# Two attention stages of a two-block transformer: the matmuls of an even and an odd head put next to each other in TensorE's queue

## The reference

```
# block 1: LayerNorm, projection, two attentions of 8 heads each (head width 64), gated mix
s = einsum('bwhd,bkwjhd->bhwkj', q, k_neighbours) * scale + bias     # neighbourhood, 8 heads
s = where(|i-j| <= 128, q.k * scale, -1e30); softmax with a sink logit  # windowed, 8 heads
mixed = sigmoid(ga) * (y_na @ w_na) + sigmoid(gb) * (y_swa @ w_swa)
# then FFN (4096), pooling mixer, convolutional GLU FFN (2816)
# block 2: 16 query heads on 4 key/value heads, causal window of 128, sinks
p = softmax(where(valid, q.k * scale, -1e30) with sink);  o = p @ v;  o @ w_o
# then a second convolutional GLU FFN
```

## Time and profile before

| | |
|---|---|
| median of 3 runs | 1015.7 us (1015.56 to 1016.41) |
| profiled execution | span 1013.8 us from the first to the last instruction; no time of its own is listed beside the span |
| PE busy | 925.0 us, 91% of the span |
| DVE, ACT, POOL busy | 652.8, 476.3, 191.3 us |
| chain that ended last | PE 77%, DVE 14% |
| stage 1 of attention | about 79.8 to 168.2 us |
| stage 2 of attention | about 707.1 to 772.2 us |

### The profile page before, as it was taken

The page is one execution under the profiler, slowest core; times in us unless marked ns, Lnnn a source line. Parts: engine busy times, 40 slices in busy tenths (PEclk is TensorE's granted clock), DMA queues, the critical chain, the costliest instruction groups (busy, mean ns, idle before and its releaser), DMA issues.

```text
span 1013.8 us, 17618 instructions
## 1 busy us (share of the span) xinstructions
PE 925.0 (91%) x7016; PEld 877.8 (87%) x7016; DVE 652.8 (64%) x864; ACT 476.3 (47%) x669; POOL 191.3 (19%) x166
## 2 busy tenths in 40 slices
PE   5898999979999999678999999869998699999995
PEld 5897878879999999568999999858677699999994
DVE  6636554767455454757776767587764867667675
ACT  4554464325444444344655454452555355545541
POOL 0501120025000000233121212431230411212131
PEclk9999999988999999778999999979899799999996
DMA  9651233443554555212454545315212145545411
GB/s 291 238 206 43 83 125 126 151 163 125 189 185 166 181 191 188 102 42 84 150 194 175 190 168 200 126 61 188 84 43 84 63 150 204 189 176 180 175 67 42
DMA packets 21842, 146.69 MB, mean 145 GB/s; under 512 B 2336, under 2 KB 3488, under 8 KB 4640
## 3 DMA queue, kind: packets, MB, share of 16 engines
q1 hardware_dynamic: 21648, 145.44, 40.2%
q10 hardware_dynamic: 144, 0.56, 0.2%
HBM read 144.94 MB, written 1.05 MB: 144 GB/s over the span
## 4 chain that ended last, share of the span: by engine, by line
PE 77%; DVE 14%; ACT 3%; issue 3%; DMA 2%; POOL 1%; DVEq 0%; ACTq 0%; SPq 0%; POOLq 0%
PE up L885 15%; PE up L886 14%; PE up L887 14%; PE down L885 7%; PE down L886 7%; PE down L887 7%; PE down L1024 3%; DVE w_lo L1311 2%; DVE region L1676 2%; DMA w<-w_stream 2%; PE down L1045 1%; DVE x_lo L1548 1%; PE aux L1045 1%; PE down L1034 1%; ACT w_hi L603 1%
## 5 line engine op out<-in xcount | busy, mean ns | idle before, releaser
L885 PE MATMUL up<-x_lo,w_hi 128*128 128x256 f32 x1360 | 391.8, 288 | 9.1 <-DVE w_lo L1311 8.7
L886 PE MATMUL up<-x_hi,w_hi 128*128 128x256 f32 x1360 | 387.1, 285 | 0.0
L887 PE MATMUL up<-x_hi,w_lo 128*128 128x256 f32 x1360 | 387.0, 285 | 0.0
L1311 DVE TENSOR_TENSOR w_lo<-w,w_hi 128x2048 fp32r<-128x2048 f32 x130 | 298.8, 2300 | 87.3 <-ACT w_hi L603 87.1
L603 ACT ACTIVATE w_hi<-w 128x2048 fp32r<-128x2048 f32 x134 | 254.9, 1904 | 74.9 <-PE down L887 42.2
L885 PEld LDWEIGHTS up<-x_lo,w_hi 128*128 128x128 f32 x1360 | 263.1, 193 | 20.3 <-DVE w_lo L1311 9.9
L886 PEld LDWEIGHTS up<-x_hi,w_hi 128*128 128x128 f32 x1360 | 263.4, 194 | 0.0
L887 PEld LDWEIGHTS up<-x_hi,w_lo 128*128 128x128 f32 x1360 | 263.3, 194 | 0.0
L885 PE MATMUL down<-mid_lo,w_hi 128*128 128x256 f32 x608 | 173.9, 286 | 10.0 <-DVE mid_lo L1685 10.0
L886 PE MATMUL down<-mid_hi,w_hi 128*128 128x256 f32 x608 | 173.4, 285 | 0.0
L887 PE MATMUL down<-mid_hi,w_lo 128*128 128x256 f32 x608 | 173.3, 285 | 0.0
(11 more groups left out here) (182 smaller groups left out, 971.8 us busy)
## 6 DMA issues: line engine op xcount, KB each, us to landing
w<-w_stream SPq DMA_DIRECT2D x134, 1024.0 KB, 4.8
region<-rpb SPq DMA_DIRECT2D x2, 768.0 KB, 18.7
gates<-x_in SPq DMA_DIRECT2D x2, 512.0 KB, 4.2
result<-gates SPq DMA_DIRECT2D x4, 256.0 KB, 2.0
con<-consts SPq DMA_DIRECT2D x1, 801.0 KB, 12.6
gates<-bands ACTq DMA_DIRECT2D x1, 544.0 KB, 3.8
par<-params SPq DMA_DIRECT2D x1, 293.0 KB, 7.5
probs<-positions SPq DMA_DIRECT2D x1, 128.0 KB, 14.4
```

The source lines that it names most:

```text
L885: m(out_ap, w_hi[slot][:, w_cols:w_cols + P], xl, start=first, stop=False, skip_group_check=True)
L886: m(out_ap, w_hi[slot][:, w_cols:w_cols + P], xh, start=False, stop=False, skip_group_check=True)
L887: return m(out_ap, w_lo[slot][:, w_cols:w_cols + P], xh, start=False, stop=last, skip_group_check=True)
L1311: v.tensor_tensor(w_lo[s][:, :], w32[s][:, :], w_hi[s][:, :].bitcast(F32), ALU.subtract)\
```

## The change

`score` and `attend` become `score_pair` and `attend_pair`: one call does an even head h and the odd head h+1, and their matmuls alternate call by call, one for the upper half, one for the lower. The pair of scores waits for both banks (`s_ready` at h, where the even head alone waited for h-1), and the pair of attends waits for the turned probabilities of both heads. In the queue the pair of scores h+2 and h+3 stands where the score of the even head h+2 stood; the score of the odd head that stood one head later is gone from there. The pair of attends stands behind the turn of an even head h and does h-2 and h-1. The other engines' code is not touched.

```
-            def score(h, q_tile, k_tile, half, plan):
+            def score_pair(h, q_tile, k_tile, plan):
                 if h >= 2:
-                    pe.wait_ge(s_ready, h - 1)
-                rows_ = slice(half * HD, (half + 1) * HD)
+                    pe.wait_ge(s_ready, h)
                 for k, (col, t, keys) in enumerate(plan):
-                    ins = m(down[h % 2][:, col:col + keys], proj[rows_, q_tile, t * P:(t + 1) * P],
-                            proj[rows_, k_tile, 0:keys], start=(k == 0), stop=True, skip_group_check=True)
-                ins.then_inc(s_done, 1)
+                    for half in range(2):
+                        rows_ = slice(half * HD, (half + 1) * HD)
+                        ins = m(down[half][:, col:col + keys], proj[rows_, q_tile, t * P:(t + 1) * P],
+                                proj[rows_, k_tile, 0:keys], start=(k == 0), stop=True, skip_group_check=True)
+                        if k == len(plan) - 1:
+                            ins.then_inc(s_done, 1)
-            def attend(h, step, fill, half, v, plan):
-                pe.wait_ge(pt_ready, h + 1)
-                if half == 0 and step // 2 >= 2:
-                    pe.wait_ge(x_ready, DC * fill + step // 2 - 1)
+            def attend_pair(h, chunk, fill, v, plan):
+                pe.wait_ge(pt_ready, h + 2)
+                if chunk >= 2:
+                    pe.wait_ge(x_ready, DC * fill + chunk - 1)
                 for k, (kc, src, width, q0) in enumerate(plan):
-                    ins = m(bank[half * HD:(half + 1) * HD, q0:q0 + width], v(kc), probs_t[h % 2][:, src:src + width],
-                            start=(k == 0), stop=(k == len(plan) - 1), skip_group_check=True)
-                ins.then_inc(o_done, 1)
+                    for half in range(2):
+                        ins = m(bank[half * HD:(half + 1) * HD, q0:q0 + width], v(half, kc),
+                                probs_t[half][:, src:src + width], start=(k == 0), stop=(k == len(plan) - 1),
+                                skip_group_check=True)
+                        if k == len(plan) - 1:
+                            ins.then_inc(o_done, 1)
...
             score1(0)
-            score1(1)
             gate_tile(1)
             for h in range(16):
-                if h + 2 < 16:
+                if h % 2 == 0 and h + 2 < 16:
                     score1(h + 2)
...
                 turn(h, full_turn)
-                if h:
-                    attend1(h - 1)
-            attend1(15)
+                if h % 2 == 0 and h:
+                    attend1(h - 2)
+            attend1(14)
...
             score2(0)
-            score2(1)
             for h in range(16):
-                if h + 2 < 16 and h:
+                if h % 2 == 0 and h + 2 < 16 and h:
                     score2(h + 2)
...
                 turn(16 + h, causal_turn)
-                if h:
-                    attend2(h - 1)
-            attend2(15)
+                if h % 2 == 0 and h:
+                    attend2(h - 2)
+            attend2(14)
```

More of the change, by code:

```diff
@@ L1035, in turn @@
                 ins.then_inc(pt_done, 1)
-            def attend(h, step, fill, half, v, plan):
-                pe.wait_ge(pt_ready, h + 1)
-                if half == 0 and step // 2 >= 2:
-                    pe.wait_ge(x_ready, DC * fill + step // 2 - 1)
-                bank = (down[3], aux)[(step // 2) % 2]
-                for k, (kc, src, width, q0) in enumerate(plan):
-                    ins = m(bank[half * HD:(half + 1) * HD, q0:q0 + width], v(kc), probs_t[h % 2][:, src:src + width],
-                            start=(k == 0), stop=(k == len(plan) - 1), skip_group_check=True)
-                ins.then_inc(o_done, 1)
+            def attend_pair(h, chunk, fill, v, plan):
+                pe.wait_ge(pt_ready, h + 2)
+                if chunk >= 2:
+                    pe.wait_ge(x_ready, DC * fill + chunk - 1)
+                bank = (down[3], aux)[chunk % 2]
+                for k, (kc, src, width, q0) in enumerate(plan):
+                    for half in range(2):
[4 more added lines that the diff above has]
+                            ins.then_inc(o_done, 1)
             full = [(0, 0, T), (T, 1, T)]
@@ L1058, in score1 @@
                 if h < 8:
-                    score(h, h // 2, 4 + h // 2, h % 2, full)
+                    score_pair(h, h // 2, 4 + h // 2, full)
                 else:
-                    score(h, 12 + (h - 8) // 2, 16, h % 2, full)
+                    score_pair(h, 12 + (h - 8) // 2, 16, full)
             def attend1(h):
@@ L1066, in attend1, with v @@
                     pe.wait_ge(rot_read, 3)
-                def v(kc):
+                def v(half, kc):
                     if h < 8:
-                        return v_tok[:, kc, h * HD:(h + 1) * HD]
-                    return v_tok_swa[:, kc, (h % 2) * HD:(h % 2 + 1) * HD]
-                attend(h, h, X_O1, h % 2, v, full_attend)
+                        return v_tok[:, kc, (h + half) * HD:(h + half + 1) * HD]
+                    return v_tok_swa[:, kc, half * HD:(half + 1) * HD]
+                attend_pair(h, h // 2, X_O1, v, full_attend)
             score1(0)
-            score1(1)
             gate_tile(1)
             for h in range(16):
-                if h + 2 < 16:
+                if h % 2 == 0 and h + 2 < 16:
                     score1(h + 2)
@@ L1229, in score2, with v @@
                     pe.wait_ge(rot_ready, 3 + 2 + h // 4)
-                score(16 + h, 4 + h // 2, h // 8, h % 2, causal)
+                score_pair(16 + h, 4 + h // 2, h // 8, causal)
             def attend2(h):
-                kv = 2 * (h // 8) + h % 2
-                attend(16 + h, h, X_O2, h % 2, lambda kc: v_tok2[:, kc, kv * HD:(kv + 1) * HD], causal_attend)
+                def v(half, kc):
+                    kv = 2 * (h // 8) + half
+                    return v_tok2[:, kc, kv * HD:(kv + 1) * HD]
+                attend_pair(16 + h, h // 2, X_O2, v, causal_attend)
             def out_chunk(u, c):
```

## The result

The changed kernel took 1018.4 us (median of 20 runs, 1016.0 to 1022.1) beside 1016.1 us for the kernel before (20 runs, 1014.6 to 1019.7): a ratio of 1.0021, 95% interval 1.0011 to 1.0031, about 2.1 us slower (the medians themselves differ by 2.3). The forecast was 1020.7, 5.0 us slower. The sign is right, the size is less than half.

A forecast was written before the change was run, and what follows sets the result against it. TensorE's queue was taken to bound the kernel, with a ring of waits replacing it in stage 1. Order -0.7 and -3.2, clock falls +5.9 and +3.0, sum +5.0 on the median 1015.7: 1020.7 us, range 1011 to 1029.

The forecast's parts named there:

- Pair of scores in 1.14: TensorE, score blocks: eight passes for two heads take 1.14 us, four of one head 1.13, so the second head is free.
- pair of attends in 1.01 net: TensorE, attend blocks: the second head is free, 1.01 us per pair; bound 1.87 if none of it is free.
- TensorE's own sum: Stage 1: 2.07 us saved per pair, 11.13 becomes 9.06; both stages together 26 us, which would give 989.7.
- The ring: Stage 1: score pair waits for VectorE's odd-head scores, behind split and attends; pairs 10.83 or 11.02 us apart, waits 1.75 or 1.9.
- the walk: Stage 1 loop timed from one score pair through TensorE, ScalarE and VectorE: 11.02 us windowed, with two hand-overs of 0.04.
- What would show it: List of trace signs; among them VectorE's wait before `x_lo` shorter and none between split and scores.
- The clock: TensorE falls to half clock after new waits, 1.48 us each: four falls, +5.9, in stage 1; two more, +3.0, in stage 2.
- Stage 2, order: Stage 2: the ring, 5.4 us, lies under TensorE's 5.56 in the later part, so the last two pairs gain: -3.2 us.
- columns serial: Rival, chance 0.10: column halves do not overlap, attend pairs 0.86 us longer in stage 1, 0.65 in stage 2; total 1031.7.
- the full gain: Rival, chance 0.08 for all or most of it: TensorE's queue stays the bound, the full 26 us, 989.7.
- the clock that holds: Rival, chance 0.20: no added clock falls, only the order counts, -3.9 us, 1011.8, faster.
- the case between: Chance 0.12: two to three clock falls in the stages, the kernel stays within 0.2% (2 us).

The follow-up runs named there:

- the filled kernel: Changed kernel plus twelve extra matmuls, results overwritten, ahead of each of five waiting score pairs in stage 1: 1016.5 us, ratio 1.0006 to the kernel before.
- the blocked kernel: Changed kernel with all matmuls of the even head, then all of the odd, instead of alternating; timed twice: 1020.2 and 1020.8 us, ratios 1.0043 and 1.0047.

## Why the prediction came out as it did

- Pair of scores in 1.14, pair of attends in 1.01 net: right. Attend to the next tile takes 1.01 with eight passes (109.58 to 110.59) as with four.
- TensorE's own sum of 9.06 per pair: right, seen once the ring is gone (9.10, 9.05, 9.10 in three kernels).
- The ring: right in mechanism and nearly in size. Forecast two pairs at 10.83 and two at 11.02, measured 10.91, 10.99, 11.09 and 11.09 (94.11, 105.01, 116.00, 127.10; 137.82, 148.91, taken before rounding). The scores of the odd head end at 115.85 and TensorE starts at 116.00: the hand-over is 0.15, where the walk had 0.04. That is +0.4 in stage 1, with +0.1 at its start and +0.1 at its end, +0.6 in all. It was the place of VectorE's copy out of PSUM that TensorE waited for, not its length: it takes 0.68 us before and after, and with the split behind it the wait is gone.
- One sign in "What would show it" was wrong: VectorE's wait before `x_lo` became longer, 4.97, and 4.71 for a windowed pair (145.63), against 3.61, since all of it now hangs on the pair of attends.
- The clock is the step that failed. For stage 1 the prediction says "I take four falls, 5.9", for stage 2 "I take two falls more than now, 3.0"; the profile has one and one, 1.5 and 1.5. In stage 1 it is across the pair with the missing tile (127.10 to 137.82 is 10.72, forecast 9.25, +1.5; without the fall, in the filled kernel, 9.38). Three other waits of 1.74, 1.83 and 1.92 left the clock at 1.00. I had counted any wait longer than those with a fall behind them in the profile of before as nearly sure to bring one; most of them did not.
- That it isn't six in the typical execution either is shown by the mean granted clock of all runs: 0.942 to 0.947 in the 29 of the changed kernel (medians 0.944 and 0.945), median 0.948 in 20 of the kernel before. Six more stretches as that at 729.08, 3.42 us at half clock, would bring 0.948 to 0.938, an estimate; two bring it to 0.945. No execution was under 0.942.
- Stage 2, order: forecast -3.2, measured about -1.6. The stage is -0.1 in all, and the one fall more, in the tile from 728.75 to 733.21 (4.46 in place of 2.98), is +1.5 of it. I had let both last pairs run free, 1.65 each. From 754.00 to 759.70 it is 5.70, a gain of 1.5 on 7.21; but from the last scores to the first product behind the stage it is 12.92 (759.70 to 772.62) against 13.37 (758.82 to 772.19), a gain of 0.45: waits of 1.02 and 0.58 for ScalarE took the rest.
- The sign was luck in part. Order and clock were forecast at -3.9 and +8.9, and the profile has -1.7 and +3.0: both too large, one against the other. With the two falls that came, the prediction's own sum would have been -0.9, faster, and the kernel was slower.
- Sum by the profile: -0.7 + 0.6 + 1.5 in stage 1, -1.6 + 1.5 in stage 2, +1.3. All runs say 2.1 (1.1 to 3.1). The rest is likely clock falls too: of the changed kernel's 20 executions the six at a mean clock of 0.942 have a median of 1020.3 us, the six at 0.947 one of 1017.6. But the profiled one, at 0.945, took only 1016.0, so the mean clock alone does not give the time; where the falls of the slower executions lie no trace shows.
- The rivals: columns serial and the full gain are excluded, and so is the clock that holds. What came true is the case between, "two to three falls": two falls beyond those of before in the stages, and 0.21% slower. It had a chance of 0.12, and should have had most of that of the four to six falls.

## What to carry to other kernels

When a change makes the bounding engine's blocks shorter, walk the whole loop from its next wait through the in-order queues of the other engines: here 2 us per pair were won in the array and lost to one copy and one weight split that stood ahead of the release. Taking the odd head's scores ahead of the split turned 0.2% slower into 1.1% faster in one stage and 1.2 to 1.3% in both, and with the missing tile at another head it is 1.5%. Try such a change one half at a time: here either half alone was a gain of 0.2 to 0.4%, and the two together a loss. A clock fall is to be priced as a chance for each wait, not as certain from some length on.

## What was not expected of the hardware

- Matmuls on the two halves of the columns (128 rows x 64 columns) overlap as fully as those on the two halves of the rows: eight passes in 1.08 us, in alternating and in blocked order. The rows do not name the head of a pass, but the four passes of one head alone take as long, so in the blocked order the odd head's first, fifth in the queue, has to start beside the even head's first, ahead of the three between them. "TensorE: Matmul & The Clock Gate" of the Trainium skill, "Part 3: Packing small matmuls", has matmuls start and end strictly in program order; no run here bears that out for different halves.
- GpSimd's normalisation of two blocks (L527) took 2.79 us at 729.11 in the changed kernel, beside VectorE's 2.27 us split of a weight unit that began at 728.93, and 0.83 at 732.94, when the split was over. The first of the two blocks takes 2.33 us at each of the two meetings with a split in the changed kernel (729.11, 747.34) and in the one before (728.45, 744.61), and 0.37 or 0.38 everywhere else in stage 2, also beside VectorE's scores. Both kernels have it, so it is no part of the difference.
- A wait of 1.9 us is followed by a fall of the clock sometimes only. Neither its length nor the code tells when: in the second timing of the blocked kernel the clock fell behind the waits of 1.82 at 116.43 and 1.91 at 150.78, in the first, the same code, it did not behind those of 1.82 at 117.80 and 1.92 at 152.20.
